# A fused residual block: c loaded as one row, step sizes behind h, another order before the first P6

## The reference

```python
mod = silu(c) @ w_ada + b_ada                       # c: one row of 1024
shift, scale, gate = split(mod, 3)
h = rmsnorm(x, norm_pre) * (1 + scale) + shift
u_pool, z_pool, u_ssm, z_ssm, g_pool, g_ssm = split(h @ w_in, ...)
...
dt = exp(log_dt)                                    # step sizes of the states
abar = exp(lam_re * dt) * (cos(lam_im * dt) + i sin(lam_im * dt))
...                                                 # pooling mixer, state-space mixer, GLU
out = (sigmoid(g_pool) * (y_pool @ w_bp) + sigmoid(g_ssm) * (y_ssm @ w_bs)) @ w_out
return x + gate * rmsnorm(out, norm_post)
```

## Time and profile before

| | before |
|---|---|
| median of 3 runs | 934.12 us |
| the profiled execution | 933.93 us |
| its span | 932.1 us |
| PE busy | 909.8 us, 98% |
| DVE busy | 726.2 us, 78% |
| ACT busy | 389.0 us, 42% |
| POOL busy | 45.3 us, 5% |

### The profile page before, as it was taken

One profiled execution on the slowest core, in us unless ns is written; L12 is line 12 of the kernel. 1 busy time (PEld: TensorE's weight loads), 2 busy tenths in 40 slices (PEclk: granted clock), 3 DMA queues, 4 the chain that ended last, 5 costly groups with the idle time before them and its releaser, 6 DMA issues.

```text
span 932.1 us, 11810 instructions
## 1 busy us (share of the span) xinstructions
PE 909.8 (98%) x4312; PEld 763.3 (82%) x4312; DVE 726.2 (78%) x1057; ACT 389.0 (42%) x534; POOL 45.3 (5%) x82
## 2 busy tenths in 40 slices
PE   3999999999999999999999999999999999999996
PEld 3888888888888888888888888888888888887885
DVE  5988899887777888546789589948468786679977
ACT  5841353343444444344544353623144460136443
POOL 0019900000000000000000000000000000000000
PEclk9999999999999999999999999999999999999999
DMA  9843265545455364437799676476355268454233
GB/s 351 313 142 106 118 228 184 163 159 158 161 195 184 143 225 175 180 75 199 191 265 244 132 198 156 132 247 231 114 226 203 95 225 320 182 198 154 76 106 135
DMA packets 97449, 169.85 MB, mean 182 GB/s; under 512 B 38768, under 2 KB 55280, under 8 KB 97392
## 3 DMA queue, kind: packets, MB, share of 16 engines
q1 hardware_dynamic: 87600, 164.55, 54.1%
q10 hardware_dynamic: 9792, 4.56, 1.9%
HBM read 121.88 MB, written 47.19 MB: 181 GB/s over the span
## 4 chain that ended last, share of the span: by engine, by line
PE 96%; DVE 1%; ACT 1%; DMA 1%; issue 0%; ACTq 0%; DVEq 0%
PE ps L2537 41%; PE ps L2691 32%; PE psb L2691 13%; PE ps L2762 2%; PE psb L2742 2%; PE psb L2751 2%; PE psa L2730 2%; PE psa L2617 1%; PE psa L2537 1%; DMA par_are<-in_a_re 1%; PE psb L2617 0%; PE psb L2567 0%; ACT gt L1196 0%; DVE mod_out L1747 0%; PE psa L2567 0%
## 5 line engine op out<-in xcount | busy, mean ns | idle before, releaser
L2537 PE MATMUL ps<-bop,w_hi 128*128 128x512 f32 x864 | 232.2, 391 | 0.8 <-DVE bop L1789 0.8
L2537 PEld LDWEIGHTS ps<-bop,w_hi 128*128 128x128 f32 x864 | 161.2, 188 | 33.7 <-issue 0.9
L2537 PE MATMUL ps<-bop,w_lo 128*128 128x512 f32 x432 | 133.0, 389 | 0.0
L2537 PEld LDWEIGHTS ps<-bop,w_lo 128*128 128x128 f32 x432 | 81.1, 188 | 17.0
L2691 PE MATMUL ps<-bop,r_hi 128*128 128x512 f32 x272 | 83.7, 389 | 0.0
L1743 DVE TENSOR_TENSOR w_lo<-raw,w_hi 128x1024 fp32r<-128x1024 f32 x35 | 43.4, 1239 | 37.8 <-ACT w_hi L1182 37.5
L1182 ACT ACTIVATE w_hi<-raw 128x1024 fp32r<-128x1024 f32 x35 | 36.9, 1053 | 76.6 <-PE ps L2537 68.4
L2691 PEld LDWEIGHTS ps<-bop,r_hi 128*128 128x128 f32 x272 | 51.1, 188 | 10.6
L2691 PE MATMUL ps<-t_hi,r_hi 128*128 128x512 f32 x140 | 55.1, 393 | 0.0
L2691 PE MATMUL ps<-t_hi,r_lo 128*128 128x512 f32 x140 | 54.6, 390 | 0.0
L2691 PE MATMUL ps<-t_lo,r_hi 128*128 128x512 f32 x140 | 54.5, 389 | 0.0
(11 more groups left out here) (464 smaller groups left out, 1889.0 us busy)
## 6 DMA issues: line engine op xcount, KB each, us to landing
raw<-in_wstream SPq DMA_DIRECT2D x36, 512.0 KB, 5.4
pair_raw<-in_wstream SPq DMA_DIRECT2D x30, 512.0 KB, 4.2
ada<-in_w_ada SPq DMA_DIRECT2D x16, 512.0 KB, 11.3
x_tok<-in_x SPq DMA_DIRECT2D x8, 512.0 KB, 7.0
gs_d<-gt SPq DMA_DIRECT2D x8, 512.0 KB, 4.9
win_d<-win_new SPq DMA_DIRECT2D x8, 512.0 KB, 2.7
wout_d<-wout_new SPq DMA_DIRECT2D x8, 512.0 KB, 3.8
wout<-wout_d SPq DMA_DIRECT2D x8, 512.0 KB, 4.8
```

Source lines behind the costliest of these rows:

```text
L2537: last = mm(ps[slot(u)][:, f * HALF:f * HALF + HALF], a[:, k, :], b(k, f), start=k == order[0] and q == 0, stop=k == order[-1] and q == 2)
```

## The change

c is loaded as one row by ACT's queue instead of 128 equal rows by SP's. ACT computes silu of that row before the first tile of x and loads the Sqrt table between its second and third tile. PE multiplies a column of ones by the row into `psa`, DVE copies the result to `silu_row`, and the first transposes into `psa` wait for the copy. `plain_angles` moves on DVE from the start to behind the last `split_h`. In `step`, PE makes high·high, low·high and only then high·low, so the first four of six matmuls wait for `h_hi_done` and the last two for `h_done`. Before the first P6, DVE makes the sums and P6's low part ahead of `t_low(3)`, and PE's P6 waits for the sums of h tile by tile.

```diff
@@ ones and semaphores
+        ones = at("ones", [P, P], w_lo_at)
+        ones_made, silu_spread, silu_copied = sem("ones_made"), sem("silu_spread"), sem("silu_copied")
@@ sync
-            sp.dma_start(silu_row[:, :], c_d).then_inc(c_in, 16)
@@ scalar
+            act.dma_start(silu_row[0:1, :], c_d[0:1, :]).then_inc(c_in, 16)
             act.dma_start(par["ldt"], log_dt_d).then_inc(par_in, 16)
...
+            act.wait_ge(c_in, 16)
+            fn(silu_row[0:1, :], silu_row[0:1, :], ACT.Silu).then_inc(silu_ready, 1)
             act.wait_ge(cols_in, 16)
-            fn(stat[:, 5, 0:1], cols[:, 0:1], ACT.Sqrt, scale=0.0)
...
                 for t in tiles:
+                    if t == 3:
+                        fn(stat[:, 5, 0:1], cols[:, 0:1], ACT.Sqrt, scale=0.0)
...
-            act.wait_ge(c_in, 16)
-            fn(silu_row[:, :], silu_row[:, :], ACT.Silu).then_inc(silu_ready, 1)
@@ vector
-            dve.wait_ge(par_in, 16 * 3)
-            plain_angles(steps)
+            nc.vector.memset(ones[0:1, :], 1.0).then_inc(ones_made, 1)
+            dve.wait_ge(silu_spread, 1)
+            nc.vector.tensor_copy(silu_row[:, :], psa[:, :]).then_inc(silu_copied, 1)
...
-            dve.wait_ge(silu_ready, 1)
+            dve.wait_ge(silu_copied, 1)
...
             split_h(KT - 1)
+            dve.wait_ge(par_in, 16 * 3)
+            plain_angles(steps)
             reduced_angles(steps)
...
             t_low(2)
-            t_low(3)
             sum1(0)
             sum2(0)
             sum4(0)
-            for i in (P6, P5, P3, P4):
+            pair_low(0, P6)
+            t_low(3)
+            for i in (P5, P3, P4):
                 pair_low(0, i)
@@ tensor, step
-                pe.wait_ge(h_done, k + 1)
-                last = k_step(u, k, *h)
+                pe.wait_ge(h_hi_done, k + 1)
+                hi, lo = (wx_hi, wx_lo) if n == 2 else (w_hi[n % 2], w_lo[n % 2])
+                for q, (a, part) in enumerate(((hi, h[0]), (lo, h[0]), (hi, h[1]))):
+                    if q == 2:
+                        pe.wait_ge(h_done, k + 1)
+                    for f in range(2):
+                        last = mm(ps[slot(u)][:, f * HALF:f * HALF + HALF], a[:, k, :], part(k, f),
+                                  start=k == 0 and q == 0, stop=k == KT - 1 and q == 2)
@@ tensor, head and pairs
+            pe.wait_ge(ones_made, 1)
+            pe.wait_ge(silu_ready, 1)
+            for f in range(2):
+                last = mm(psa[:, f * HALF:f * HALF + HALF], ones[0:1, :], silu_row[0:1, f * HALF:f * HALF + HALF],
+                          start=True, stop=True)
+            last.then_inc(silu_spread, 1)
...
+                    if k == 3 and 0 in tiles:
+                        pe.wait_ge(silu_copied, 1)
...
                 for k in range(4):
+                    if (j, i) == (0, P6):
+                        pe.wait_ge(t_done, k + 1)
...
-                if j == 0:
-                    pe.wait_ge(t_done, 4)
```

## The result

In six runs each, one after the other on the same chip, the changed kernel takes 938.24 us (936.63 to 939.38) and the kernel before 934.20 (933.94 to 934.70): ratio 1.0042, 95% interval 1.0031 to 1.0052. It is slower by 4.0 us, at the upper end of the range. The profiled execution took 939.14 us, with a span of 937.5.

What follows compares the result with a forecast made beforehand. PE was taken as the bound, busy 909.8 of 932.1 us. Profiled 933.93 plus 1.35 (product 3) and 0.9 (next pair's P1) made 936.2, the median 0.19 higher: 936.4 us; eight-in-ten range 934.6 to 938.3.

Steps and rivals of the forecast that it cites:

- the rival's clock term: Behind the wait before product 3: the clock falls, up to 1.9 us more, 938.3 us; chance 0.16.
- The head: Start of the kernel: first diagonals 1.5 us earlier, sums with w_ada 1.3 us earlier, near 18.4 (ends 0 and 2.1).
- Product 3: PE waits about 3 us near 62.6 for `split_lo(3)` and starts 1.3 us later, at 65.7; +1.35 in the sum.
- The second pair: At the next pair's P1, PE idles 0.9 us for a low part delayed by `t_low` (ends 0 and 1.3).
- the paragraph on the clock: At PE's 3 us wait near 62.6: a fall to 1.2 GHz would cost up to 1.9 us; not in the sum.
- The prediction's own sign of being wrong: After product 3's start: products after 65.7 at twice their spacing for some microseconds would show the forecast wrong.
- Behind it on DVE: After product 3: rotation table and coefficients' store 3.2 us later, next low parts have spare time; costed at nothing.
- the rival with the head's gain kept: At product 3: `split_lo(3)` is ready when PE comes, PE keeps 1.3 to 2.1 us, 932.3 us; chance 0.10.
- Low weights second: In the steps of h: removes most of PE's 0.8 us wait; PE 1.3 to 2.1 us earlier towards product 3.

Runs made afterwards that it cites:

- the step sizes late alone: The kernel before with only `plain_angles` and its wait moved behind the last `split_h`: 938.20 us, ratio 1.0056.
- the run with the weight tile first: The changed kernel with `split_lo(3)` put right behind `plain_angles`, ahead of `reduced_angles` and `sine`: 940.62 us, ratio 1.0072.
- PE kept busy: The changed kernel with 12 products of 512 columns put into TensorE's wait before product 3, outputs unchanged: 938.66 us, ratio 1.0048.

## Why the prediction was right and wrong

**The time** is in the range, but by a rival, not by the forecast: 936.4 and the rival's clock term of up to 1.9 made 938.3, against 938.24. That it agrees to 0.1 is partly luck: three of the six runs took 936.63 to 937.33 and three 939.14 to 939.38, the latter above the range, and the median lies between the two groups.

**The head** was right: first transposes near 13 (12.94), sums with w_ada at 18.4 (18.21), `plain_angles` 53.5 to 58 (53.74 to 58.20).

**Product 3** was right: start at 65.7 (65.88), +1.35 (+1.48), a wait of about 3 us (2.79).

**The second pair** was right in size (0.9; 0.85 measured) and, for the table load, in mechanism: without it the wait goes. That the place of `t_low(3)` is needed too was only argued: the run with the old order (the step sizes late alone) has no wait there, but no table load either.

**The step that failed** is the paragraph on the clock: "Three microseconds lie between", and the time was then summed with nothing for it, at a chance of 0.16. Measured is 1.77, and in the two other profiles of the changed kernel 1.74 and 2.56 (4.46 and 5.28 for twelve records, less 2.72); behind the 2.41 us wait of the step sizes late alone it is 1.7, and filling PE's wait took it away. The prediction's own sign of being wrong, products behind 65.7 at twice their spacing, came true: four records take 1.91 at 67.92 and 1.07 at full pace. The warning of the Trainium skill that was set against the rows there ("TensorE: Matmul & The Clock Gate", section "HAM oscillation") was the better guide: the trace agrees with it here (0.61 behind 2.79 us), though the waits in that section's example are longer.

**Behind it on DVE**, "I cost this at nothing; its cover is a few tenths" came true, but only because PE was 3.25 us late itself while the store of the coefficients was 3.6 late (119.07). With PE 1.64 earlier and the store 2.66 later (121.73) it was a wait of 2.73 with half pace behind it. Thus the rival with the head's gain kept could not have paid 1.3 to 2.1 us with the angles where the change puts them, even if `split_lo(3)` had been ready: it was, in the run with the weight tile first, and that took 940.62. Its table of rotations starts 0.93 later than the changed kernel's (71.65 against 70.72); taken off the 3.35 us at P1, that leaves 2.4 (an estimate).

**Low weights second** was counted as a gain of PE on its way to product 3. It is one, of 0.56 us alone, 0.2 of it passes the first P6, which had no cover in the kernel before, and the time shows nothing of it.

## What to carry to other kernels

When a step moves, follow every chain that starts from its result, each to the place where the bound engine waits, and not only the first; two chains with the same small cover hide each other until one is mended. A wait on TensorE is priced as the wait and, where the granted clock of the stretch behind it falls, the slow pace too (here 1.7 us and more behind waits of 2.41 us and longer, nothing behind those of 2.12 and shorter). Work that no engine has room for late can go to an engine that idles early, even at three times its duration (14.3 us on GpSimd instead of 4.47 on VectorE).

## What was not expected of the hardware

**The clock.** Behind waits of 2.41, 2.72, 2.73, 2.76, 2.79, 3.35 and 3.60 us the granted clock of the next 3.8 to 5.3 us was 0.50 to 0.62, or twelve records took 4.4 us or more (the lower of its two levels, 1.2 GHz, for most of it); behind 0.65, 0.80, 0.96, 1.59 and 2.12 us it stayed at 1.00. At the start of the kernel before, where the pace is half as well, the same view gives 1.00 from 14.4 to 19.0: that slow start is not in this record, so the pace must be read beside it.

**GpSimd and VectorE stretch each other.** From the first step of the rotations to the coefficients' store it is 48.4 us in the changed kernel and 51.0 with PE kept busy, where VectorE paused less (busy 42.3 and 44.7 of the same 48.3 us, 70.7 to 119.0). The longest step of the latter, and VectorE's beside it:

```profile
117.78 2.67 POOL L620 TENSOR_TENSOR coef<-coef 128x256 f32<-128x256 f32 x1
```

```profile
117.12 2.73 DVE L1842 TENSOR_TENSOR t_lo<-t_f,t_hi 128x2048 fp32r<-128x2048 f32 x1
```

The Trainium skill, "SBUF — State Buffer", section "Who interferes with whom", says that a VectorE instruction with two inputs in SBUF and a GpSimd instruction that reads SBUF contend; both rows are of that kind, and the trace agrees. In the kernel before, a GpSimd step of that kind and size starts at 88.40, while VectorE still waits for ACT, and takes 0.72; there it is VectorE's low part, begun at 88.49, that takes 1.72 instead of 1.22. That a VectorE that waits less delays what GpSimd makes fits these rows and the two lengths; no run varied VectorE's pauses alone.
